# One layer of a streaming encoder on one core: G projected half by half, a shorter routing chain with more filler products, gate products moved behind the first gate projection

## What is computed

```python
h = rmsnorm(x, norm_mix_g); z = h @ w_in          # G, R, U, Q, K, V column blocks
x = x + concat(gla, pool, diff_attention) @ w_out
x = x + memory_attend(rmsnorm(x, norm_mem_g), mk, mv, w_mem_q, w_mem_o)
t = rmsnorm(x, norm_ffn_g)
g_prob = softmax(t @ w_rg + b_rg); g_top = argmax(g_prob)          # 4 groups
e_in = (t @ w_re + b_re)[group g_top]                               # 4 experts in each
top_v, top_i = top_k(softmax(e_in), 2); top_v = top_v / sum(top_v)
for e in range(16):
    y = (silu(t @ w_g[e]) * (t @ w_u[e])) @ w_d[e]
    out = out + gate[:, e] * y                     # gate = p(group) * top_v, 0 elsewhere
x = rmsnorm(x + out, final_norm_g)
```

## Time and profile before

| | |
|---|---|
| median of three runs | 733.04 us |
| the profiled execution | 732.52 us |
| its span, first to last instruction | 730.6 us |
| TensorE busy, share of the span | 676.3 us, 93% |
| VectorE | 522.6 us, 72% |
| ScalarE | 425.0 us, 58% |
| POOL | 142.1 us, 19% |
| mean granted TensorE clock | 0.973 |
| DMA | 161.23 MB, mean 221 GB/s |

### The profile page before, as it was taken

One profiled execution on the slowest core, in us unless ns is written; L12 is line 12 of the kernel. 1 busy time (PEld: TensorE's weight loads), 2 busy tenths in 40 slices (PEclk: granted clock), 3 DMA queues, 4 the chain that ended last, 5 costly groups with the idle time before them and its releaser, 6 DMA issues.

```text
span 730.6 us, 9430 instructions
## 1 busy us (share of the span) xinstructions
PE 676.3 (93%) x3469; PEld 544.4 (75%) x3469; DVE 522.6 (72%) x697; ACT 425.0 (58%) x602; POOL 142.1 (19%) x160
## 2 busy tenths in 40 slices
PE   4999999998999999889999499999999999999991
PEld 3898887776666776778888278888888888888861
DVE  4436655565877674656457778899999999988883
ACT  6646643244664443454233358887777788888880
POOL 4102850011001011000001302222222122222134
PEclk9999999999999999999999579999999999999996
DMA  8623232403771000310094869999999999999863
GB/s 307 220 74 148 113 146 78 155 0 131 266 299 69 1 1 31 125 46 1 1 359 150 343 242 359 369 382 366 383 374 375 383 369 375 382 371 386 307 218 121
DMA packets 32867, 161.23 MB, mean 221 GB/s; under 512 B 6189, under 2 KB 6523, under 8 KB 18108
## 3 DMA queue, kind: packets, MB, share of 16 engines
q1 hardware_dynamic: 23392, 140.39, 50.3%
q0 software_dynamic: 5344, 10.27, 5.2%
q10 hardware_dynamic: 4092, 10.08, 3.8%
HBM read 149.59 MB, written 20.03 MB: 232 GB/s over the span
## 4 chain that ended last, share of the span: by engine, by line
PE 75%; DVE 12%; DMA 5%; issue 2%; ACT 2%; POOL 1%; SPq 1%; ACTq 0%; POOLq 0%; DVEq 0%
PE pj L2110 43%; PE scores L2110 14%; PE tr_v L2110 10%; DVE wl L1412 4%; PE tr_a L2118 2%; PE scores L2490 2%; PE tr_v L2118 2%; DMA acc_rows<-y,idx_sb 1%; DMA xs_next<-acc_rows,idx_sb 1%; PE tr_a L2519 1%; DMA xT_raw<-in_xT 1%; DVE w_lo L1441 1%; DVE hid L1412 1%; DMA xg<-h_rows,idx_sb 1%; POOL rs L749 1%
## 5 line engine op out<-in xcount | busy, mean ns | idle before, releaser
L1412 DVE TENSOR_TENSOR wl<-moe_raw,wh 128x2048 fp32r<-128x2048 f32 x96 | 218.5, 2290 | 28.2 <-ACT wh L901 26.2
L901 ACT ACTIVATE wh<-moe_raw 128x2048 fp32r<-128x2048 f32 x96 | 182.3, 1919 | 37.8 <-PE pj L2110 12.6
L2110 PE MATMUL pj<-w_hi,xT_hi 128*128 128x512 f32 (+2 forms) x192 | 70.7, 368 | 9.1 <-DVE w_lo L1441 8.3
L747 POOL TENSOR_SCALAR rs<-stat 128x1 f32<-128x1 f32 (+4 forms) x31 | 10.7, 344 | 320.6 <-DVE stat L1623 158.6
L2110 PE MATMUL pj<-w_hi,xT_lo 128*128 128x512 f32 (+2 forms) x192 | 68.9, 359 | 0.0
L2110 PE MATMUL pj<-w_lo,xT_hi 128*128 128x512 f32 (+2 forms) x192 | 68.8, 358 | 0.0
L802 POOL DMA_INDIRECT acc_rows<-y,idx_sb x14 | 22.3, 1591 | 207.7 <-ACT y L1335 193.6
L2110 PE MATMUL pj<-wh,xgh 128*128 128x512 f32 x128 | 52.8, 412 | 1.4 <-DVE xgl L1412 1.4
L1441 DVE SCALAR_TENSOR_TENSOR w_lo<-raw,pack_a,w_hi 128x512 fp32r<-128x512 f32 (+2 forms) x64 | 43.8, 745 | 11.8 <-ACT w_hi L945 11.8
L2110 PE MATMUL tr_v<-wh,xgh 128*128 128x512 f32 x128 | 51.1, 400 | 0.0
L2110 PE MATMUL pj<-wh,xgl 128*128 128x512 f32 x128 | 51.0, 398 | 0.0
(11 more groups left out here) (416 smaller groups left out, 1483.5 us busy)
## 6 DMA issues: line engine op xcount, KB each, us to landing
moe_raw<-in_w_exp_gate SPq DMA_DIRECT2D x32, 1024.0 KB, 8.4
moe_raw<-in_w_exp_up SPq DMA_DIRECT2D x32, 1024.0 KB, 9.9
moe_raw<-in_w_exp_down SPq DMA_DIRECT2D x32, 1024.0 KB, 10.0
raw<-in_dense SPq DMA_DIRECT2D x16, 1024.0 KB, 6.0
raw<-in_dense SPq DMA_DIRECT2D x8, 256.0 KB, 6.4
x_rows<-in_x_prompt SPq DMA_DIRECT2D x4, 512.0 KB, 11.6
xw<-in_x_prompt ACTq DMA_DIRECT2D x1, 2048.0 KB, 8.4
h_rows<-h ACTq DMA_DIRECT2D x4, 512.0 KB, 3.8
```

What stands on the lines that cost most here:

```text
L747: link(pool.tensor_scalar(rs[rows, n, cs], stat[rows, n, cs], EPS, None, ALU.add))
L901: act.activation(wh[s4][:, :], moe_raw[n % RING][:, :], ACT.Copy).then_inc(hi_done, 1)
L1412: return dve.tensor_tensor(out, a, b, op)
L2110: return pe.matmul(out, lhsT, rhs, start=start, stop=stop, skip_group_check=True)
```

## The change

At the start, G's tiles 0 and 1 are projected on the first half of the features, then both on the second half, then tile 2 half by half; four banks instead of two hold the results. x tiles 0 to 2 are loaded and split in halves, the rows of x are loaded behind x tile 3, the transposes of G move back by one to two tiles, and all but 27 columns of `pack_a` are loaded after the split of x tile 4.

In the routing, the logits of tiles 2 to 4 are computed transposed (weights stationary, tokens moving), copied by ScalarE and transposed back. VectorE searches the group and the experts in one search of 25 rows of four, multiplies the choices by the group before they are summed, does the positions of both choices with one product and one sum from PSUM, and each `placed` with one operation. The positions take eleven products. Operations that only the gates need come behind the list. POOL clears the gather buffer after the last memory output and `xs` after the first two gathers. SP's queue waits for the first gather before unit 6. Fillers are 17 ahead of the positions, 6 ahead of the entries and 22 behind them. The gate products of the routing (`gates`) come behind the first expert's gate projection, VectorE's part of them behind the split of x, and the gate projection waits for one half of x at a time.

```diff
-    plan = [((b, t), row_reader(t)) for b, _, _ in IN_BLOCKS[:-1] for t in range(TILES)] + [(("Q", t), "A") for t in range(2)]
+    plan = [(("G", t), row_reader(t), (0, 1, 2, 3, 0)[t]) for t in range(TILES)]
+    plan += [((b, t), row_reader(t)) for b, _, _ in IN_BLOCKS[1:-1] for t in range(TILES)] + [(("Q", t), "A") for t in range(2)]
...
+    plan += [(("lt", t), "A") for t in range(2, TILES)]
...
+        pj_more = [sc[:, 1024:1536], sc[:, 1536:2048]]
+        pj_of = lambda key: (pj + pj_more)[PJ[key][3]]
...
-            for n in range(2):
-                ks = slice(4 * n, 4 * n + 4)
-                sp.dma_start(xT_raw[:, 0, ks, :], A["xT"][0][:, ks, :]).then_inc(x0_in[n], 16)
+            def x_half(t, g):
+                ks = slice(4 * g, 4 * g + 4)
+                sp.dma_start(xT_raw[:, t, ks, :], A["xT"][t][:, ks, :]).then_inc(xh_in[t][g], 16)
+
+            def quarter(n, k):
+                c = slice(512 * k, 512 * k + 512)
+                sp.dma_start(raw[:, n, c], unit(n)[:, c]).then_inc(part_in[n][k], 16)
+
+            for g in range(2):
+                x_half(0, g)
                 for k in range(4):
-                    c = slice(512 * k, 512 * k + 512)
-                    sp.dma_start(raw[:, n, c], unit(n)[:, c]).then_inc(part_in[n][k], 16)
-            for t in range(1, 4):
-                x_load(t)
-                rows_load(t - 1)
+                    quarter(g, k)
+                    if (g, k) == (0, 2):
+                        x_half(1, 0)
+            x_half(1, 1)
+            x_half(2, 0)
+            x_half(2, 1)
+            x_load(3)
+            rows_load(0)
+            rows_load(1)
+            x_load(4)
+            rows_load(2)
             dense_load(2)
-            x_load(4)
             rows_load(3)
             dense_load(3)
             rows_load(4)
...
                     elif n < RING:
+                        sp.wait_ge(xg_in[0], 16)
                         sp.wait_ge(acc_out, 16 * TILES)
...
-            pool.wait_ge(chosen_ready, 1)
+            pj_read(pool, ("w_mem_o", 1, TILES - 1))
             pool.memset(xg[:, :, :], 0.0).then_inc(xg_clear, 1)
-            pool.memset(xs[:, :], 0.0).then_inc(xg_clear, 1)
-            pool.wait_ge(xg_clear, 2)
+            pool.wait_ge(xg_clear, 1)
             pj_read(pool, ("entries",))
...
+            pool.memset(xs[:, :], 0.0).then_inc(xg_clear, 1)
+            pool.wait_ge(xg_clear, 2)
...
-            x0_high(0)
+            x_half_high(0, 0)
             act.wait_ge(gains_in, 16)
             w_high(0)
-            x0_high(1)
+            x_half_high(1, 0)
+            x_half_high(0, 1)
             w_high(1)
+            x_half_high(1, 1)
+            for g in range(2):
+                x_half_high(2, g)
+            x_high(3)
             act.wait_ge(consts, 1)
             for t in range(2):
-                x_high(t + 1)
                 x_square(t)
+            x_high(4)
+            act.dma_start(pack_a[:, 27:], A["pack_a"][:, 27:]).then_inc(pack_in, 16)
             act.dma_start(pack_b[:, :], A["pack_b"]).then_inc(params_in, 16)
             act.dma_start(wa2[:, :], A["w_gla_a2"][0]).then_inc(params_in, 16)
...
+            def logits_out(t):
+                act.wait_ge(sc_full, SC[("lt", t)][0] + 1)
+                act.activation(lgT[:, t - 2, 0:ROWS[t]], sc[0:20, 512 * (t - 2):512 * (t - 2) + ROWS[t]], ACT.Copy)\
+                    .then_inc(sc_act, 1)
+
             x2_out(TILES - 2)
             x2_square(TILES - 1)
+            logits_out(2)
+            x2_out(TILES - 1)
             h3_out_of(TILES - 2)
-            x2_out(TILES - 1)
+            logits_out(3)
+            logits_out(4)
             h3_out_of(TILES - 1)
             for j in (-1, 0, 1):
                 split_hi(0, 0, j)
...
+            x_half_low(0, 0, 1)
+            w_low(0)
+            x_half_low(1, 0, 2)
+            x_half_low(0, 1, 3)
+            w_low(1)
+            x_half_low(1, 1, 4)
+            for g in range(2):
+                x_half_low(2, g, 5 + g)
+            x_low(3)
...
             x2_T(TILES - 2)
+            x2_T(TILES - 1)
             logits(2)
             moe_input(TILES - 2)
-            x2_T(TILES - 1)
+            moe_input(TILES - 1)
             logits(3)
-            moe_input(TILES - 1)
...
+            all5 = hot5.rearrange("p (t g i) -> p t g i", g=5, i=4)
+            group, group_max, best = all5[:, :, 0, :], in_fives(m5)[:, :, 0], in_fives(m5)[:, :, 1:5]
+            first_best(lg[:, :, :].rearrange("p t (g i) -> p t g i", g=5), in_fives(m5), in_fives(k5), all5, rank_5)
+            link(dve.scalar_tensor_tensor(out=by_group(r80[0]), in0=all5[:, :, 1:5, :], scalar=-1e30, in1=ev,
+                                          op0=ALU.mult, op1=ALU.add))
+            tt(hot1, all5[:, :, 1:5, :], bc(group, 4), ALU.mult)
...
+            link(tt(hot2, hot2, bc(group, 4), ALU.mult))
+            tt(chosen[:, :, :], r80[1], r80[2], ALU.add).then_inc(chosen_ready, 1)
+
+            for i in range(2):
+                ins = tt(held[:, i], r80[i + 1].unsqueeze(2).to_broadcast([P, TILES, 2, E]), bc(entry[:, :, :], E), ALU.mult)
+            link(ins)
+
+            dve.wait_ge(pj_full, PJ[("pos",)][0] + 1)
+            both = scratch[:, 340:500].rearrange("p (i n) -> p i n", i=2)
+            at_pos = pj[PJ[("pos",)][3]][:, 0:80].unsqueeze(1).to_broadcast([P, 2, 80])
+            tt(r160.rearrange("p (i n) -> p i n", i=2), both, at_pos, ALU.mult).then_inc(pj_dve, 1)
+            dve.wait_ge(pj_dve, PJ[("pos",)][2] + 1)
+            link(dve.tensor_reduce(scratch[:, 2740:2750], r160.rearrange("p (n e) -> p n e", e=E), AX.X, ALU.add))
+            for i in range(2):
+                tt(placed[:, i], lane[:, :].unsqueeze(1).to_broadcast([P, TILES, P]), bc(posi[i], P), ALU.is_equal)\
+                    .then_inc(place_ready, 1)
+            tt(r20[1], lg[:, :, 0:4], bc(group_max, 4), ALU.subtract).then_inc(route_arg, 1)
+            link(tt(r20[3], r20[3], best, ALU.subtract))
+
+            dve.wait_ge(pj_full, PJ[("entries",)][0] + 1)
+            parts = pj[PJ[("entries",)][3]][:, 0:2 * E].rearrange("p (c e) -> p c e", c=2)
+            link(dve.tensor_scalar(listed, parts[:, 0], -64.0, float(EMPTY), ALU.mult, ALU.add))
+            tt(idx_sb[:, :], listed, parts[:, 1], ALU.subtract).then_inc(pj_dve, 1)
+
+            link(tt(r20[3], r20[3], group, ALU.mult))
             dve.tensor_reduce(r5[3], r20[3], AX.X, ALU.add).then_inc(route_arg, 1)
...
+            def gates_held():
+                for i in range(2):
+                    tt(gheld[:, i, :, 0:3, :], r80[i + 1].unsqueeze(2).to_broadcast([P, TILES, 3, E]),
+                       bc(gpart[:, :, i, :].rearrange("p c t -> p t c"), E), ALU.mult)
+                    ins = tt(gheld[:, i, :, 3, :], r80[i + 1], chosen[:, :, E - 1:E].to_broadcast([P, TILES, E]), ALU.mult)
+                ins.then_inc(gheld_ready, 1)
+                dve.tensor_copy(tokid[:, :, :, 1].bitcast(F32), gate[:, :, :])
+
...
+            gates_held()
...
                 split_lo(0, 0, j)
+                if j == 1:
+                    gates_out()
...
+            for part in range(2):
+                for t in range(2):
+                    pe.wait_ge(xT_lo_done, 2 * part + t + 1)
+                    project(("G", t), t, *x_block(t), BLOCK_UNITS["G"], WIDTH["G"], part)
+            for part in range(2):
+                pe.wait_ge(xT_lo_done, 5 + part)
+                project(("G", 2), 2, *x_block(2), BLOCK_UNITS["G"], WIDTH["G"], part)
+            for t in range(3, TILES):
+                rows_T("G", t - 3, 2)
+                pe.wait_ge(xT_lo_done, t + 4)
+                project(("G", t), t, *x_block(t), BLOCK_UNITS["G"], WIDTH["G"])
+            rows_T("G", 2, 2)
+            in_block("R", 0, {0: lambda: rows_T("G", 3, 2), 1: lambda: rows_T("G", 4, 2)})
...
+            def router_T(t):
+                sc_read(pe, ("mem", TILES - 1))
+                for g in range(2):
+                    tr_read(pe, ("x2", t, g))
+                out = sc[0:20, 512 * (t - 2):512 * (t - 2) + ROWS[t]]
+                for k in range(KB):
+                    ins = mm(out, wr[:, k, :], hT[:, t % 2, k, 0:ROWS[t]], k == 0, k == KB - 1)
+                ins.then_inc(sc_full, 1)
+
+            def logits_T(t):
+                j = claim("pj", PJ, PJ_KEYS, ("router", t), pj_act, pj_dve)
+                sc_read(pe, ("lt", t))
+                pe.transpose(pj[j][0:ROWS[t], 0:20], lgT[:, t - 2, 0:ROWS[t]], ident[0:20, 0:20]).then_inc(pj_full, 1)
+
+            def keep_warm(n):
+
+                pe.wait_ge(hi_done, 1)
+                for _ in range(n):
+                    mm(py[1], wh[0][:, 0:P], wh[0][:, 0:512], True, True)
+
             x2_T(TILES - 2)
-            router(2)
+            router_T(2)
             x2_T(TILES - 1)
-            router(3)
-            router(4)
-
+            logits_T(2)
+            router_T(3)
+            router_T(4)
+            logits_T(3)
```

(31 more changed lines are left out.)

120 lines of the change are left out of this document (36 added, 84 removed).

## The result

The changed kernel takes 723.85 us (median of four, 723.23 to 726.27) beside 732.56 for the kernel before (four runs by now): a ratio of 0.9881, 95% interval 0.9841 to 0.9921, or 8.7 us less. The forecast was 724.5. The profiled execution took 723.23 us, its span 721.2 instead of 730.6.

The account below looks back on a forecast made before the run. TensorE was taken to bound the kernel, so gains come only where it waits or runs at half clock. Terms -0.9 - 4.4 - 1.5 - 3.0 + 0.7 + 1.0 sum to -8.1 us: 724.5 us, range 721 to 729.

Parts of the forecast that it names:

- Start: Kernel start: projecting G half by half removes TensorE's wait for x tile 1, -0.9 us (bounds -1.2 to +0.5).
- The rival of no gain at the start: Start: the wait only moves to tile 1's second half or a late weight quarter; 725.4 us, chance 0.09.
- Logits: Routing: transposed logits of tiles 2 to 4, with a copy and small transpose, +0.1 us (bounds -0.3 and +1.0).
- Search: Routing: one search on 100 elements replaces group and expert searches; choice written at 405.3 us instead of 406.1.
- Choice to list: Routing, from expert choice to row list: 4.0 us instead of 6.2, the list standing 3.0 earlier, at 409.3.
- Gather: First gather, issue to landing: 4.4 us instead of 5.81, landing at 414.6 instead of 419.05, -4.4 us.
- Gate products moved: First expert: ten routing gate products, formerly in TensorE's idle time, now stand between gate projection and transposes, +0.7 us.
- VectorE's debt: First expert: VectorE owes 16.2 us of work, so the hidden product comes late, +1.0 us once (bounds 0 and +2).
- Fillers in the way: Routing: at half clock from the first filler on, fillers delay the chain; slower, 737 us, chance 0.03.
- clock falling in the routing: Between choice and list TensorE's clock falls to half, giving back about 3 us; 727.5 us, chance 0.20.
- Held loads, free: SP's queue: units 6, 7 and 8 start 7 us later, behind the gather wait, at no cost.
- Rival B: First experts wait for the delayed weights, giving back up to 7.1 us; 731.5 us, no change, chance 0.06.

Follow-up runs that it names:

- e12: The kernel before plus only SyncE's wait that holds the last four early expert-weight loads until the first gather has landed; 730.06 us, ratio 0.9968.
- e11: The kernel before with only the fillers added (17, 6, and 6 ahead of and 16 behind the gate products); 728.63 us, ratio 0.9965.
- e5: The changed kernel with GpSimd's clearing of xs moved to its end and held gate loads and products put ahead of the low half of x; 724.70 us.
- e10: Second measurement of the changed kernel with GpSimd's clearing moved to its end and the gates ahead of the low half of x; 724.95 us, ratio 0.9889.

## Why the prediction was right

- **Start, -0.9.** The wait that was named is gone. The two profiles beside each other give -0.87, the means over 14 profiles -1.3. The rival of no gain at the start fell.
- **Logits, +0.1.** From the square to the last logit it is 0.38 longer (55.18 less 54.80), within the bounds. The products of tiles 3 and 4 took 2.76 us (forecast 2.8). But I let VectorE's order set the end, and it was TensorE's path: its products ended at 398.06, ScalarE copied (398.09), the transpose came at 398.44, and VectorE, done with `h3`, waited 0.17 us for it.
- **Search.** 4.91 us from the last logit to the choice became 4.02: -0.9 as forecast. With the logits, the choice gained 0.5 instead of 0.8.
- **Choice to list.** 2.29 us shorter, forecast 2.2. The rule that a two-input operation cannot read two elements a cycle (the Trainium skill, "VectorE: DVE Perf Modes", "Why `tensor_tensor` can't do 2×_2P or 4×") did not turn the sum: ten one-input operations took 2.05 us against 1.56, so for this size the fixed part of each weighs more than the rate.
- **Gather.** 4.42 us, forecast 4.4, and 4.21 to 4.42 in the eight other profiles with the wait. The estimate of 3.2 us from the Trainium skill ("DMA: Bandwidth & Descriptors", "Anatomy of one DMA — SWDGE (gpsimd) path") was 1.0 to 1.2 too low in every one of them, even in the changed kernel, where from 407 to 409 us no packet moved on any DMA engine.
- **Landing to product** -1.26 (forecast -1.5), and **gate products** -2.80 (-3.0).
- **Gate products moved and VectorE's debt:** forecast +0.7 and +1.0, together +1.18 measured. The debt is the mis-sized term: 0.5, not 1.0. And its cause was in part another than VectorE's load of splits, since moving the clearing and the gates took all of it away.
- **Fillers in the way, clock falling in the routing:** neither came. The clock was full in 396 to 424 us, and the 17 fillers ended (402.70) before the choice was written (402.92).
- **Held loads, free.** This term was wrong by a little. In the two profiles of the changed kernel ScalarE never waits for weights behind 400 us, but the part behind expert 2 is 0.3 to 0.5 us longer than in the kernel before, and up to 2.7 in others with the wait (under e12). Rival B came in small part.

Two attributions behind the sum were not right as put. I had put 4.5 us to the clock and the fillers; without them only 2.15 were lost. In the kernel before the clock fell twice, the second time in the wait for the gather, and that made the gate products slow. A shorter gather alone (e12) or fillers alone (e11) keep the clock up there, so neither carries the whole. And "held loads: free" looked at their wait only as a possible cost. I took 4.4 for the gather on its account, with 5.8 as the bad end, a row of a kernel in which the gather met the end of those loads. At its new time it meets all of them, and takes 8.81.

The 1.8 us that the first pair of profiles shows beyond the forecast are a draw of the two executions. The parts themselves add up to 7.7 to 8.1 us (0.9 to 1.3 at the start, 0.5 to the choice, 6.6 behind it, less 0.3), where 8.1 was forecast and 8.4 to 8.7 measured by the ratios.

## What to carry to other kernels

A transfer on the critical path that is moved to an earlier time meets other traffic there: look up what the queues issue around the new time, not the old one, and hold it back if nobody waits for it; then look at the end of the loop too, whether the delay was made up. Slow clock, slow gather and idle TensorE feed each other, so what each remedy is worth alone does not add up, and only taking one out of the whole shows what it still carries. To judge a few tenths of a per cent, cut the profiles at fixed marks: where the clock was full, stretches of the middle repeated to 0.05 us here, while timed runs of one kernel spread over 2.5 to 8 us. Where the clock fell, two profiles of one kernel differed by 1.9 us in one stretch.

## What the runs showed of the hardware

- Short stretches of 3 to 4 us at half clock come in some executions of a program and not in others, at one or two of three places (about 178, 296 and 316 us), and cost 1.6 to 1.8 us each here.
- A gather of 512 KB from GpSimd's queue took 4.2 to 4.4 us with the weight loads held back, 5.1 to 6.5 with some of them under way, and 8.8 when it was issued 2.3 us behind the first of four loads of 1 MB.
- Those four loads, held back some 8 us near 410 us, were followed 250 us later by waits of ScalarE for weights of 0.5 to 2.3 us in five profiles of nine, and in none of five without the hold.
- A VectorE cast of ten elements a partition took 1.70 us instead of 0.17 while GpSimd issued an indirect transfer and cleared 128x1024, and ended with the clearing in every kernel that has it there. With the clearing moved away (e5, e10) it took 0.17 again, beside the same issue. That a cast can be held until a GpSimd instruction ends is stated by the Trainium skill ("SBUF — State Buffer", "Who interferes with whom": the two engines share a pair of ports, and one holds it for its whole instruction); the two-input operations beside it, to which the page gives no such wait against a clearing, ran at their usual 0.17 us up to 409.56. By the records the cast began 0.7 us before the clearing did, which the page's rule does not explain and no run here settles.
